# All page loads of the first stage issued by GpSimd's queue instead of half by GpSimd and half by SyncE

## The chip, the cores and the metric

The kernel runs on one core of one Trainium2 chip. The metric is the device time of one execution in microseconds (us). Engines are named as the profile names them: PE is TensorE's matmul, PEld its weight load, DVE is VectorE, ACT is ScalarE, POOL is GpSimd, SP is SyncE. SP does no arithmetic here: its program only waits on semaphores and issues DMAs. All DMAs, whoever issues them, are carried out by the core's 16 DMA engines; the profile calls SP's queue q1, POOL's queue q0 and ACT's queue q10.

## What is computed (the reference)

One inference step of two layers: a convolution mixer, then an attention layer over a paged cache. Only the past cache and the mixer's input product matter here; the reference, cut to that:

```python
def conv_mixer(x, state, w_in, ...):            # layer 0
    h = x @ w_in + b_in                         # 1024 -> 3 x 2048
    ...                                         # gate, 31 taps, layer norm, gate, product

def compress(kseq, pe, w1, b1, w2):             # layer 1, of keys and of values
    chunks = kseq.reshape(B, nchunk, 16, N_KV, HEAD_DIM)
    parts = einsum("bcsgd,jsdh->jbcgh", chunks, w1r)
    ...
    return einsum("bcgh,hd->bcgd", silu(h), w2)

past = cache_kv[page_table].reshape(8, 2048, 4, N_KV, HEAD_DIM)   # 8 sequences of 16 pages
kc = compress(past[:, :, 0], ...)
vc = compress(past[:, :, 1], ...)
cache_win_sample = concatenate([cache_win, new])[:, 8:]           # windows moved on by 8 rows
```

## The kernel before, in words

Each engine's program is written out by hand, with semaphores between them. The first stage runs 17 units, `u` from 0 to 16. In unit `u` PE multiplies channel tile `u` of the mixer (64 matmuls at L1385, weights `wi` of buffer `u % 2`), and beside it compresses "half sequence" `cu = u - 1`: the keys (even `cu`) or the values (odd `cu`) of one of the 8 sequences. A unit has 8 steps `q`. In each step ACT first gathers rows of the half sequence from the landing buffer `xc` (`regroup`, L791), PE transposes them (`turn_chunk`, L1428), ACT copies the result out of PSUM (`chunk_out`, L781), and PE multiplies it by the compressor's weights (L1456). ACT works two steps ahead: step 6 of unit `u` already gathers step 0 of the half sequence `cu = u`. That first gather waits for all 16 pages of the half sequence. Within a step PE's order is fixed: transposes, then the mixer's part, then the compressor's part, so PE stands still when ACT does.

A half sequence is 16 page loads of 128 KB, each to 8 partitions of `xc`, which has two buffers (`cu % 2`). A buffer is free once ACT has gathered the last step of `cu - 2` (`rg_ready`, 8 counts for a half sequence). Before the change two queues load it. POOL issues pages 8 to 15 as soon as the buffer is free (L700 to L708). SP issues pages 0 to 7 (`load_chunks`, L481), for `cu` 0 and 1 ahead of its loop, and then inside its loop over `u`. In the loop, L517 on, SP waits for the end of PE's unit `u` (`a_ps`), loads the weights and the state of unit `u + 2` (`load_mixer`, L471 and L473), stores the states of unit `u - 1` (L492, L493), waits for the buffer and issues its 8 pages of `cu = u + 1` (L485). In turn `u = 2` it issues two DRAM to DRAM copies after that: L531, 1408 KB of `state_conv`, and L533, 8064 KB of `cache_win`. What SP issues behind them runs in the same queue behind them.

At the very start ACT's queue loads the inputs, SP's queue loads the page table, `wi` of unit 0 and ten small tensors (L497 to L505, semaphore `s_small`), then the compressor's weights (L509), then pages 0 to 7 of `cu = 0`, `wi` of unit 1 and pages 0 to 7 of `cu = 1`. POOL's queue carries pages 8 to 15 of both from the start on. PE needs the ten small tensors before its first transposes of parameters (L1377), and these before unit 0.

Of the kernel before, what the change touches and what calls it, by code (L numbers as in the profile page):

```python
# [18 lines left out]
NB, TS = 8, 8  # L19
# [10 lines left out]
NPG = PAST // PAGE  # L30
STR = 16
# [18 lines left out]
STEPS = 8  # L50
# [45 lines left out]
def build_program(nc, x_prompt, x_sample, state_conv, cache_kv, cache_win, page_table,  # L96
# [4 lines left out]
    with ctx:  # L101
        def sem(name):
            return ctx.enter_context(nc.semaphore(name))

        arena = ctx.enter_context(nc.sbuf_tensor("arena", [P, ARENA], F32))
        pages = ctx.enter_context(nc.sbuf_tensor("pages", [1, NB * NPG], I32))
        bank = [ctx.enter_context(nc.psum_tensor(f"bank{i}", [P, 512], F32)) for i in range(8)]

        def at(kib, n):

            o = int(kib * 256)
            assert o + n <= ARENA
            return arena[:, o:o + n]
# [24 lines left out]
        xc = at(142, 2 * 4096).rearrange("p (c s f) -> p c s f", c=2, s=STR)  # L138
# [103 lines left out]
        s_cb = sem("s_cb")  # L242
        s_pg = sem("s_pg")
        xc_in = [sem(f"xc_in{c}") for c in range(2)]
        xq_in = [sem(f"xq_in{c}") for c in range(2)]
        rg_ready = sem("rg_ready")
        turn_ps = sem("turn_ps")
        turn_ev = sem("turn_ev")
# [215 lines left out]
        def _(sp):  # L464
            sp.dma_start(pages[:, :], page_table.rearrange("(o b) n -> o (b n)", o=1)).then_inc(s_pg, 16)

            def load_mixer(ct):
                c = ct % 2
                for a, part in ((0, 1), (1, 0)):
                    col = part * DIN + ct * P  # L470
                    sp.dma_start(wi[:, c, a], conv_w_in[0].rearrange("(k p) n -> p k n", p=P)[:, :, col:col + P]  # L471
                                 ).then_inc(wi_in[c], 16)
                sp.dma_start(st[0:120, c], state_conv[0].rearrange("(h b) t n -> (b t) h n", h=2)[:, :, ct * P:(ct + 1) * P]  # L473
                             ).then_inc(wi_in[c], 16)

            def load_gate(zi):
                col = 2 * DIN + zi * P
                sp.dma_start(wz[:, zi % ZS], conv_w_in[0].rearrange("(k p) n -> p k n", p=P)[:, :, col:col + P]
                             ).then_inc(wz_in[zi % ZS], 16)

            def load_chunks(cu):  # L481
                b, s = divmod(cu, 2)
                for n in range(NPG // 2):
                    pg = sp.value_load(pages[0:1, b * NPG + n:b * NPG + n + 1], min_val=0, max_val=cache_kv.shape[1] - 1)
                    sp.dma_start(xc[n * 8:n * 8 + 8, cu % 2],  # L485
                                 cache_kv[0, bass.ds(pg, 1)].rearrange("o (c s) k g d -> (o c) s (k g d)", s=STR)[:, :, s * 256:(s + 1) * 256]
                                 ).then_inc(xc_in[cu % 2], 16)

            def store_states(ct):
                c = ct % 2  # L490
                sp.wait_ge(turn_ev, TURN["tail", ct] + 1)
                sp.dma_start(state_p[0, 0, :, ct * P:(ct + 1) * P], uo[0:30, c, 0:P]).then_inc(state_out[c], 16)  # L492
                sp.dma_start(state_s[0, :, TAPS - 1 - TS:TAPS - 1, ct * P:(ct + 1) * P], uo[0:64, c, P:256]  # L493
                             ).then_inc(state_out[c], 16)
# [12 lines left out]
            def load_compressor():  # L507
                for s in range(2):
                    sp.dma_start(wc[:, s].rearrange("p j q h -> p (j q) h"),  # L509
                                 cmp_w1[0, s].rearrange("(q e) d h -> (e d) q h", e=2)).then_inc(s_wc, 16)  # L510

            load_compressor()
            sp.wait_ge(s_pg, 16)
            load_chunks(0)
            load_mixer(1)
            load_chunks(1)
            for u in range(CT):  # L517

                sp.wait_ge(a_ps, u + 1)
                if u + 2 < CT:  # L520
                    load_mixer(u + 2)
                else:
                    for zi in (2 * (u + 2 - CT), 2 * (u + 2 - CT) + 1):
                        load_gate(zi)
                if u:
                    store_states(u - 1)
                if 1 <= u < 2 * NB - 1:
                    sp.wait_ge(rg_ready, u * STEPS)
                    load_chunks(u + 1)
                if u == 2:  # L530
                    sp.dma_start(state_s[0, :, 0:TAPS - 1 - TS].rearrange("b t n -> b (t n)"),  # L531
                                 state_conv[0, :, TS:TAPS - 1].rearrange("b t n -> b (t n)")).then_inc(s_cpy, 16)
                    sp.dma_start(win_s[0, :, 0:WIN - TS].rearrange("b t k g d -> b (t k g d)"),  # L533
                                 cache_win[0, :, TS:WIN].rearrange("b t k g d -> b (t k g d)")).then_inc(s_cpy, 16)
# [41 lines left out]
            load_permuted(0, used + 24)  # L576
            load_compressor()

            sp.wait_ge(kv_out, 64)
            for st_ in range(2):  # L580
                for g in range(NKV):
# [36 lines left out]
            for n in range(NPG):  # L618
                pg = sp.value_load(pages[0:1, n:n + 1], min_val=0, max_val=cache_kv.shape[1] - 1)
# [48 lines left out]
        def _(pool):  # L668
# [30 lines left out]
            for cu in range(2 * NB):  # L699
                b, s = divmod(cu, 2)  # L700
                if cu >= 2:

                    pool.wait_ge(rg_ready, (cu - 1) * STEPS)
                for n in range(NPG // 2, NPG):
                    pg = pool.value_load(pages[0:1, b * NPG + n:b * NPG + n + 1], min_val=0, max_val=cache_kv.shape[1] - 1)
                    pool.dma_start(xc[n * 8:n * 8 + 8, cu % 2],  # L706
                                   cache_kv[0, bass.ds(pg, 1)].rearrange("o (c s) k g d -> (o c) s (k g d)", s=STR)[:, :, s * 256:(s + 1) * 256]
                                   ).then_inc(xq_in[cu % 2], 16)  # L708

            pool.wait_ge(hp_ev, 2)  # L710
            pool.memset(vbd, 0.0).then_inc(vbd_zero, 1)
# [54 lines left out]
        def _(act):  # L766
# [16 lines left out]
            def regroup(k):  # L783
                cu, q = divmod(k, STEPS)
                if q == 0:
                    act.wait_ge(xc_in[cu % 2], cu // 2 * 128 + 128)
                    act.wait_ge(xq_in[cu % 2], cu // 2 * 128 + 128)
                if k >= 2:

                    act.wait_ge(turn_ps, TURN["chunk", (k - 2) // STEPS, (k - 2) % STEPS] + 1)  # L790
                act.copy(rg[:, k % 2].rearrange("p g (e d) -> p g e d", e=2),  # L791
                         xc[:, cu % 2, 2 * q:2 * q + 2].rearrange("p e (g d) -> p g e d", g=NKV)).then_inc(rg_ready, 1)
# [117 lines left out]
            with act.Fori(0, 2) as it:  # L910
                for t in range(TT):
                    n = ROWS[t]
# [7 lines left out]
            for t in range(TT):  # L920
                n = ROWS[t]
# [28 lines left out]
            for gp in range(2):  # L950
                with act.Fori(0, 2) as it:
                    g0 = it * 32 + gp * 64
                    for u in range(33):
                        if u < 32:
                            n = (UNITS[u][1] + 1) * P
# [5 lines left out]
                        if u >= 1:  # L961
                            v = u - 1
                            n = (UNITS[v][1] + 1) * P
# [406 lines left out]
        def _(pe):  # L1370
# [328 lines left out]
            def step(b, c, scores=True, output=True):  # L1699
# [9 lines left out]
                def turn_weights(n):  # L1709

                    if n:
                        copied_out(n - 1)
                    pe.wait_ge(e_scl, b * 2 - (1 if n < 2 else 0))
                    for t, (col, rows, _) in enumerate(groups[n]):
                        last = pe.transpose(bank[7][0:rows, t * P:(t + 1) * P], p[:, col:col + rows], ident)
                    last.then_inc(e_pp, 1)

                def weigh(n):
                    copied_out(n)
                    if n == 0:  # L1720
                        pe.wait_ge(c_stage, b)
                        pe.wait_ge(v_in[s2], (b - 1 - s2) * 24 + 48)
                        pe.wait_ge(vp_in[s2], (b - 1 - s2) * 128 + 256)

                        pe.wait_ge(e_oz, b * 4 - 3)
                    for t, (_, rows, v) in enumerate(groups[n]):
                        for g in range(2):
                            rhs = pt[0:rows, n % 4, t * P:(t + 1) * P].rearrange("p (q g m) -> p g q m", q=TS, g=2)[:, g]
                            last = pe.matmul(bank[5 + g][:, 0:64].rearrange("p (q m) -> p q m", q=TS), v[:, g * P:(g + 1) * P], rhs,  # L1729
                                             start=n == 0 and t == 0, stop=n == 6)  # L1730
                    if n == 6:
                        last.then_inc(e_pv, 1)
# [98 lines left out]
```

## Time and profile before

| | us |
|---|---|
| median of 3 runs (1782.03 to 1786.17) | 1784.23 |
| the profiled execution, device time | 1785.66 |
| its span, from first to last instruction | 1784.1 |
| PE busy | 1642.5 (92%) |
| DVE busy | 875.2 (49%) |
| ACT busy | 498.4 (28%) |
| POOL busy | 179.9 (10%) |
| page loads of the first stage issued by POOL, and by SP | 128 each, of 128 KB |
| median from issue to landing, POOL's page loads (whole kernel) | 4.4 |
| median from issue to landing, SP's page loads (whole kernel) | 2.6 |

Times in the rows are from the start of the span. The busy share of an engine is an average over stages with different limits, so each stretch is read by itself. A landing is counted by the semaphore of a transfer, to which every DMA engine that took part adds; several loads in flight count on one semaphore, so a landing says when so many counts had come in, not which page it was.

### The profile page before, as it was taken

What the parts mean: (1) busy time and instruction counts of PE and PEld (TensorE: products, weight loads), DVE (VectorE), ACT (ScalarE), POOL (GpSimd) and SP (SyncE); (2) the same over time, 40 slices, a digit from 0 to 9 for tenths busy, and PEclk for the clock granted to TensorE, in tenths of its full rate; (3) what the DMA queues carried; (4) which work ended last, traced back from release to release, by engine and by line L of the source; (5) the groups of instructions that cost most, each with busy time, mean ns of one, the idle gap of its engine ahead of it and who ended that gap; (6) DMA issues with size and microseconds to landing.
All of it is one profiled execution on the core that took longest, in us unless ns stands there. A gap on an engine that the chain in (4) does not pass through costs nothing.

```text
span 1784.1 us, 24182 instructions
## 1 busy us (share of the span) xinstructions
PE 1642.5 (92%) x7065; PEld 1070.9 (60%) x7065; DVE 875.2 (49%) x1940; ACT 498.4 (28%) x1079; POOL 179.9 (10%) x336
## 2 busy tenths in 40 slices
PE   1999749999999999999989999997999979999897
PEld 1766536666666667743433366366778747777753
DVE  0467647888788754211320010016777763454334
ACT  0134223444444422210000000022666632333100
POOL 3012101111111000000000000002000024232100
PEclk6799969999999999999999999988999999999789
DMA  9557645766766526111002256103000045554501
GB/s 157 107 94 128 223 93 86 112 93 90 107 101 88 94 86 230 48 48 47 0 6 59 54 144 136 37 3 99 2 1 2 1 141 176 176 178 143 133 36 42
DMA packets 173096, 160.56 MB, mean 90 GB/s; under 512 B 55350, under 2 KB 150969, under 8 KB 172793
## 3 DMA queue, kind: packets, MB, share of 16 engines
q1 hardware_dynamic: 154742, 119.79, 29.9%
q0 software_dynamic: 16384, 33.64, 9.2%
q10 hardware_dynamic: 1864, 5.90, 0.9%
q8 instruction: 44, 0.72, 0.2%
q14 instruction: 62, 0.51, 0.1%
HBM read 152.41 MB, written 16.38 MB: 95 GB/s over the span
## 4 chain that ended last, share of the span: by engine, by line
PE 86%; SPq 4%; DMA 3%; DVE 2%; issue 2%; ACT 1%; POOLq 0%; POOL 0%; DVEq 0%; ACTq 0%
PE bank L1385 20%; PE bank L1456 11%; PE bank L395 11%; PE bank L1729 5%; PE bank L1664 4%; PE bank L1525 4%; PE bank L1801 4%; PE bank L1537 4%; PE bank L1688 4%; PE bank L1564 3%; PE bank L1428 3%; PE bank L1773 3%; PE bank L1678 2%; SPq L471 2%; DMA arena<-in_cmp_w_dram 2%
## 5 line engine op out<-in xcount | busy, mean ns | idle before, releaser
L1385 PE MATMUL bank<-arena 128*128 128x288 f32 x1536 | 401.1, 411 | 0.0
L1385 PEld LDWEIGHTS bank<-arena 128*128 128x128 f32 x1536 | 285.7, 193 | 69.1
L1065 DVE SCALAR_TENSOR_TENSOR arena<-arena 128x512 f32<-128x512 f32 x464 | 313.8, 743 | 0.0
L1456 PE MATMUL bank<-arena 128*128 128x508 f32 x512 | 238.8, 589 | 0.0
L395 PE MATMUL bank<-arena 128*128 128x512 f32 (+3 forms) x480 | 203.4, 571 | 2.7 <-DVE arena L1140 1.1
L781 ACT COPY arena<-bank 128x512 f32<-128x512 f32 x128 | 74.8, 585 | 297.0 <-PE bank L1428 297.0
L395 PEld LDWEIGHTS bank<-arena 128*128 128x128 f32 (+1 forms) x480 | 80.1, 194 | 125.6 <-issue 119.6
L1456 PEld LDWEIGHTS bank<-arena 128*128 128x128 f32 x512 | 97.3, 190 | 74.2 <-issue 60.8
L706 POOL DMA_DIRECT2D arena<-in_cache_kv_dram x128 | 76.6, 598 | 503.1 <-issue 502.9
L1428 PEld LDWEIGHTS bank<-arena 128*128 128x128 f32 x512 | 64.6, 143 | 91.6 <-issue 57.5
L1428 PE MATMUL bank<-arena 128*128 128x128 f32 x512 | 78.0, 275 | 32.4 <-ACT arena L808 32.4
L1729 PE MATMUL bank<-arena 128*128 128x64 f32 (+2 forms) x736 | 101.9, 295 | 5.6 <-DMA arena<-in_cache_kv_dram 5.6
L1729 PEld LDWEIGHTS bank<-arena 128*128 128x128 f32 (+2 forms) x736 | 98.0, 212 | 9.1 <-issue 7.7
L1664 PE MATMUL bank<-arena 128*128 128x128 f32 (+3 forms) x256 | 97.5, 468 | 1.6 <-DVE arena L1199 1.6
L791 ACT COPY arena<-arena 128x512 f32<-128x512 f32 x128 | 79.6, 623 | 45.0 <-DMA arena<-in_cache_kv_dram 45.0
L438 DVE SCALAR_TENSOR_TENSOR arena<-arena,bank 128x512 f32<-128x512 f32 (+1 forms) x20 | 13.6, 682 | 149.2 <-PE bank L1525 64.0
L1688 PE MATMUL bank<-arena 128*128 128x64 f32 x640 | 86.4, 267 | 0.0
L1688 PEld LDWEIGHTS bank<-arena 128*128 128x128 f32 x640 | 82.0, 193 | 2.1
L759 POOL DMA_DIRECT2D arena<-in_cache_kv_dram x128 | 70.9, 554 | 99.4 <-issue 99.2
L959 ACT ACTIVATE arena<-bank,arena 128x128 f32<-128x128 f32 (+3 forms) x128 | 67.7, 529 | 46.8 <-DVE arena L1237 45.6
L1773 PE MATMUL bank<-arena 128*128 128x512 f32 x160 | 76.7, 603 | 0.0
L1525 PE MATMUL bank<-arena 128*128 128x512 f32 (+1 forms) x160 | 74.2, 608 | 1.0 <-ACT arena L850 1.0
(213 smaller groups left out, 1819.1 us busy)
## 6 DMA issues: line engine op xcount, KB each, us to landing
arena<-in_cache_kv_dram POOLq DMA_DIRECT2D x256, 128.0 KB, 4.4
arena<-in_cache_kv_dram SPq DMA_DIRECT2D x256, 128.0 KB, 2.6
arena<-in_conv_w_in_dram SPq DMA_DIRECT2D x48, 512.0 KB, 7.1
arena<-in_nsa_w_in_dram SPq DMA_DIRECT2D x64, 128.0 KB, 2.3
arena<-in_cache_win_dram SPq DMA_DIRECT2D x16, 512.0 KB, 4.9
out_dram<-in_cache_win_dram SPq DMA_DIRECT2D x1, 8064.0 KB
arena<-in_nsa_w_in_dram SPq DMA_DIRECT2D x24, 256.0 KB, 2.6
arena<-in_conv_w_out_dram SPq DMA_DIRECT2D x2, 2048.0 KB, 8.1
```

The lines of the kernel that those rows point to most:

```text
L395: ins = pe.matmul(bank[t][0:r, 0:width], lhs(k, t), slot, start=first, stop=last_k)
L706: pool.dma_start(xc[n * 8:n * 8 + 8, cu % 2], cache_kv[0, bass.ds(pg, 1)].rearrange("o (c s) k g d -> (o c) s (k g d)", s=STR)[:, :, s * 2 ...
L791: act.copy(rg[:, k % 2].rearrange("p g (e d) -> p g e d", e=2), xc[:, cu % 2, 2 * q:2 * q + 2].rearrange("p e (g d) -> p g e d", g=NKV)).t ...
L1065: taps.append(ch.mark(dve.scalar_tensor_tensor(part, src, w, part, ALU.mult, ALU.add)))
L1385: last = pe.matmul(bank[pair + h][:, 0:HALF], weights[:, k], xT[:, k, h * HALF:(h + 1) * HALF], start=k == 0, stop=k == KT - 1)
L1428: last = pe.transpose(dst[:, g * P:(g + 1) * P], rg[:, k % 2, g], ident)
L1456: last = pe.matmul(h, wc[:, s, j, q], x4[:, :, j:j + NC], start=(q == 0 and j == 0), stop=(q == STEPS - 1 and j == 1))
L1525: last = pe.matmul(bank[t][0:r, :], y[:, c, t * P:t * P + r], wo[:, c], start=c == 0, stop=c == CT - 1)
L1664: pe.matmul(bank[u % 3][:, 0:n], qs[c][:, g2, i * P:(i + 1) * P], ktp[:, br, gp, 0:n], start=True, stop=True).then_inc(u_sc, 1)
L1688: last = pe.matmul(bank[5 + v % 3][:, 0:HD], probT[:, v % 2, k * P:(k + 1) * P], kvr[:, k, col:col + HD], start=k == 0, stop=k == i)
L1729: last = pe.matmul(bank[5 + g][:, 0:64].rearrange("p (q m) -> p q m", q=TS), v[:, g * P:(g + 1) * P], rhs, start=n == 0 and t == 0, stop=n ...
L1773: last = pe.matmul(s_bank[n][:, :], qb[:, c, g], ktb[n % 2][:, g], start=g == 0, stop=g == 1)
```

## The change

SP no longer issues page loads in the first stage: `load_chunks` and its three calls are gone, with the wait for `rg_ready` in SP's loop. POOL's loop issues all 16 pages of each half sequence, for the same `cu`, after the same wait as before. All 16 loads count on one semaphore, `xc_in`, and ACT waits for it alone. SP's wait for the page table moves to a later place, ahead of its first other use of pages.

```diff
-            def load_chunks(cu):
-                b, s = divmod(cu, 2)
-                for n in range(NPG // 2):
-                    pg = sp.value_load(pages[0:1, b * NPG + n:b * NPG + n + 1], min_val=0, max_val=cache_kv.shape[1] - 1)
-                    sp.dma_start(xc[n * 8:n * 8 + 8, cu % 2], ...).then_inc(xc_in[cu % 2], 16)
...
             load_compressor()
-            sp.wait_ge(s_pg, 16)
-            load_chunks(0)
             load_mixer(1)
-            load_chunks(1)
             for u in range(CT):
...
                 if u:
                     store_states(u - 1)
-                if 1 <= u < 2 * NB - 1:
-                    sp.wait_ge(rg_ready, u * STEPS)
-                    load_chunks(u + 1)
                 if u == 2:
...
                     pool.wait_ge(rg_ready, (cu - 1) * STEPS)
-                for n in range(NPG // 2, NPG):
+                for n in range(NPG):
                     pg = pool.value_load(...)
                     pool.dma_start(xc[n * 8:n * 8 + 8, cu % 2], ...
-                                   ).then_inc(xq_in[cu % 2], 16)
+                                   ).then_inc(xc_in[cu % 2], 16)
...
                 if q == 0:
-                    act.wait_ge(xc_in[cu % 2], cu // 2 * 128 + 128)
-                    act.wait_ge(xq_in[cu % 2], cu // 2 * 128 + 128)
+                    act.wait_ge(xc_in[cu % 2], cu // 2 * 256 + 256)
```

## Rows read from the trace of the kernel before

**Rows 1.** The page: PE's busy tenths in 40 slices of the span.

```profile
PE   1999749999999999999989999997999979999897
```

**Rows 2.** The chain that ended last, 170 to 252 us: start, length, what.

```profile
178.53 33.80 SPq L471
...
212.37 10.93 SPq L473
...
240.45 4.63 DMA arena<-in_cache_kv_dram
```

**Rows 3.** Timeline of PE, 205 to 252: start, length, instructions, idle before and releaser.

```profile
209.87 2.11 PE L1385 MATMUL bank<-arena 128*128 128x288 f32 x8
211.81 1.87 PE L1456 MATMUL bank<-arena 128*128 128x508 f32 x4
246.03 1.12 PE L1428 MATMUL bank<-arena 128*128 128x128 f32 x4 [32.35 <-ACT arena L808]
246.94 3.64 PE L1385 MATMUL bank<-arena 128*128 128x288 f32 x8
```

**Rows 4.** Timeline of ACT, around 172 and 245: gathers of the pages.

```profile
172.31 0.62 ACT L791 COPY arena<-arena 128x512 f32<-128x512 f32 x1
...
245.10 0.62 ACT L791 COPY arena<-arena 128x512 f32<-128x512 f32 x1 [38.74 <-DMA arena<-in_cache_kv_dram]
```

**Rows 5.** One unit's stretch: length, busy of each engine, granted clock, DMA share, GB/s.

```profile
306.00:340.00 34.00, 34.00 (x142) 22.70 (x141) 27.92 (x42) 14.28 (x26) 4.79 (x8) 1.00 0.71 97
```

**Rows 6.** Timeline of POOL: single page loads.

```profile
26.23 0.60 POOL L706 DMA_DIRECT2D arena<-in_cache_kv_dram  x1 [0.62 <-issue]
...
135.98 0.60 POOL L706 DMA_DIRECT2D arena<-in_cache_kv_dram  x1 [24.71 <-issue]
...
144.81 0.60 POOL L706 DMA_DIRECT2D arena<-in_cache_kv_dram  x1 [0.62 <-issue]
...
169.91 0.60 POOL L706 DMA_DIRECT2D arena<-in_cache_kv_dram  x1 [24.50 <-issue]
...
312.54 0.61 POOL L706 DMA_DIRECT2D arena<-in_cache_kv_dram  x1 [2.05 <-issue]
```

**Rows 7.** Line L706 alone: its 128 loads, from issue to landing.

```profile
DMA to landing us min/median/max: 4.2/5.4/44.2
```

**Rows 8.** Timeline of SP's queue, 140 to 180.

```profile
144.13 1.05 SPq L471 DMA_DIRECT2D arena<-in_conv_w_in_dram  x2
...
151.26 15.56 SPq L485 DMA_DIRECT2D arena<-in_cache_kv_dram  x8
166.87 0.73 SPq L531 DMA_DIRECT2D out_dram<-in_state_conv_dram  x1
...
178.06 34.27 SPq L471 DMA_DIRECT2D arena<-in_conv_w_in_dram  x2
```

**Rows 9.** DMA queues, 184 to 204: packets, MB, share of 16 engines.

```profile
q1 hardware_dynamic: 65, 4.19, 48.7%
q0 software_dynamic: 65, 0.13, 1.7%
```

**Rows 10.** DMA issues, 212 to 213: count, KB, us from issue to landing.

```profile
arena<-in_state_conv_dram SPq DMA_DIRECT2D x1, 120.0 KB, 18.8
```

**Rows 11.** Stretch 151 to 155, columns as in rows 5.

```profile
151.00:155.00 4.00, 4.00 (x18) 2.59 (x17) 4.00 (x5) 1.16 (x4) 0.00 (x0) 1.00 1.09 142
```

**Rows 12.** The chain, 0 to 82 us: the wait ahead of PE's first unit.

```profile
12.41 35.01 DMA arena<-in_cmp_w_dram
```

**Rows 13.** DMA queues in 36:41.8; then q1 in 41.8:44.8; in 44.8:47.6.

```profile
q0 software_dynamic: 256, 0.42, 62.8%
q1 hardware_dynamic: 7, 0.06, 5.0%
...
q1 hardware_dynamic: 19, 0.04, 3.8%
...
q1 hardware_dynamic: 32, 0.02, 2.7%
```

More of the change, by code:

```diff
@@ L244, in build_program @@
         xc_in = [sem(f"xc_in{c}") for c in range(2)]
-        xq_in = [sem(f"xq_in{c}") for c in range(2)]
         rg_ready = sem("rg_ready")
@@ L479, in load_gate @@
                              ).then_inc(wz_in[zi % ZS], 16)
-            def load_chunks(cu):
-                b, s = divmod(cu, 2)
-                for n in range(NPG // 2):
-                    pg = sp.value_load(pages[0:1, b * NPG + n:b * NPG + n + 1], min_val=0, max_val=cache_kv.shape[1] - 1)
-                    sp.dma_start(xc[n * 8:n * 8 + 8, cu % 2],
-                                 cache_kv[0, bass.ds(pg, 1)].rearrange("o (c s) k g d -> (o c) s (k g d)", s=STR)[:, :, s * 256:(s + 1) * 256]
-                                 ).then_inc(xc_in[cu % 2], 16)
             def store_states(ct):
@@ L577, in _ @@
             load_compressor()
+            sp.wait_ge(s_pg, 16)
             sp.wait_ge(kv_out, 64)
```

## The prediction

> **What bounds the kernel now.** I read PE's slices first [rows 1]: outside the stage changes PE is at 9 tenths or more nearly everywhere, so a change of page loads can move the time only where PE has a hole. In the first stage there are two, slice 0 and slices 4 and 5. Then the table of stretches, for a unit with no hole: PE is busy 34.00 of 34 us [rows 5], though both queues load pages there. Units like this (I looked at 306 to 340 and 578 to 612) can gain nothing.
>
> The hole in slices 4 and 5 is followed back in three views. PE ends a unit's compressor part at 211.81 + 1.87 = 213.7 and then idles 32.35 us behind ACT; its next eight mixer matmuls take 3.64 us where the same eight took 2.11, the clock having dropped in the idle time [rows 3]. I price the hole at 32.35 + 2 = 34.5 us. ACT itself waited 38.74 us for pages, to 245.10 [rows 4]. So a wait of ACT costs PE about 4 us less than its length. The chain names the cause [rows 2]: SP's queue stands 33.80 us in the second weight load of L471, 10.93 us in L473, and only then issues its pages, the last landing at 245.1. SP stood because, two DMAs earlier, it had issued the copies L531 at 166.87 and L533 [rows 8], and its queue has no room until they run dry. POOL's eight pages of that half sequence had been issued from 169.91 on [rows 6].
>
> The hole in slice 0 is one wait: PE's first parameter transposes wait for the last small load, issued 12.41, landed 35.01 us later, at 47.4 [rows 12].
>
> **The change, part by part.** *SP's 128 page loads go.* A batch occupies SP for 15.56 us [rows 8], but no engine waits on SP except where it is blocked: worth nothing in an ordinary unit, and if anything else were late on SP it would now come some 17 us sooner. The three waits that move or go cost nothing: ACT's two become one on the same event, the page table landed long before.
>
> *POOL issues 16 instead of 8.* The pace is (144.81 - 135.98) / 7 = 1.26 us a load, so 16 take 20.2, and 5.4 more to land [rows 6, 7]: 25.6 us. The window is one unit of 34 us plus the 4 us from the step that frees the buffer to the step that gathers, 38 in all [rows 4 to 6]: covered, by 12 us. If that cover were gone, each us over it would cost one us in 14 units. POOL has nothing else to do until after the stage, so nothing queues behind its waits.
>
> *The copies start sooner.* Without pages SP reaches L531 right after L493, at about 150 instead of 166.87. The transfers don't start 17 us sooner, though: the DMA engines are full to 155 with SP's weights and state of unit 4 (share 1.09 in 151 to 155 [rows 11]), and POOL's eight extra pages now fall into this stretch, 8 x 1.26 = 10 us more work. So they start between 17 and 0 us sooner than now; I take 8. How the copy behaves is shown by 184 to 204 [rows 9]: in 20 us SP's queue moved 65 packets of 4.19 MB / 65 = 64.5 KB at a DMA share of about a half, eight engines, so 20 x 8 / 65 = 2.46 us a packet; and POOL's queue moved 65 as well, one for one. The 8064 KB are 128 such packets, 16 for each of eight engines: 39 us, and 1408 KB at the same rate about 7 more. An estimate from rates: they end near 219 now (a start near 170 plus 46 and some), near 211 after.
>
> *What is late then.* Unit 5 needs the weights and state of L471 and L473, still behind the copies, and the pages of `cu = 4`, now all in POOL's queue. Now L473 is issued at 212.37 and lands 18.8 later, at 231.2, 12 after the copies' end [rows 2, 10]; the same offset gives 223. The pages, issued 169.91 to 190, are held by the copy on the eight engines and flushed after it, as now the last caught one landed 44.2 us after its issue [rows 7], and I put them at the same 223. PE stands from 213.7 to 223 and pays 2 us of low clock: 11.5 us for 34.5, a gain of 23. With copies 17 sooner the loss would be 2.5 and the gain 32; not sooner at all, 21 and 13.5.
>
> *The start.* Here the extra 2 MB of pages of `cu` 0 and 1 cost. The small loads run on few engines: in 36 to 41.8, with POOL's queue full everywhere (256 packets), SP's moved 7, 0.83 us each; once POOL's pages were through, the next 5.8 us moved 19 + 32 = 51 [rows 13]. POOL issued its 16th load at 26.23 [rows 6]; after the change 16 more follow at 1.26, to about 47, so its queue stays full past 47. If all 51 packets keep alternating with POOL's at the loaded pace (5.8 x 16 engines / 256 = 0.36 us a packet for 46 small ones, 0.83 for some 5 large): 16.6 + 4.1 = 20.7 instead of 5.8, +15. If the extra pages disturbed nothing, 0; a gain is excluded, since SP's queue up to the last small load is unchanged and only meets more traffic. Many of POOL's packets are nearly empty, and the last 32 of SP's took only 2.8 / 32 = 0.09 us a turn with POOL's still among them: at the mean of 0.09 and 0.36, 46 x 0.22 + 4.1 = 14.3, +8.5. I take +9. It moves PE's whole first unit and is hidden by nothing. The compressor's weights come later by the same amount and are needed later by the same amount.
>
> Sum: +9 - 23 = -14: 1785.66 - 14 = 1771.7 for the profiled execution. The median lies 1.4 lower: 1784.2 - 14 = **1770 us**. The bounds make 1784 - 32 = 1752 to 1784 - 13.5 + 15 = 1786.
>
> One rule speaks against POOL as issuer. In POOL's rows each load takes 0.60 us with gaps of 0.62, the longest gap shown 2.05 [rows 6], while DVE is busy 27.92 of 34 us [rows 5]. The Trainium skill ("SBUF — State Buffer", section "SBUF: two separate sides", the box on DVE blocking DMA) says that a DVE operation in a two-port mode keeps GpSimd from writing the descriptors of its DMAs, and gives about 3.1 us for one that takes 0.62 alone; by that, 16 loads would take some 50 us and overrun the window by 17 us or so. The trace disagrees so far.
>
> **The rivals.** *(a) The pages of `cu = 3` are caught: slower.* They are issued from 135.98 on, after the change to about 156, and gathered at 172.31 [rows 4, 6]. A caught page has some five packets in each of the eight engines' queues (an estimate: 128 KB in packets of 4 KB over 16 engines, and its counts), each waiting for one of 2.46 us: 12 us a page. One page still queued when the copies begin is covered, two or more are not; with four, the copies' 20 packets an engine are used up, and the pages land when the copies end. That needs copies at their earliest, the full 17 us, with POOL's pages held back by the weights. Then ACT waits from 172.3 to about 206, 33.5 us, PE 29.5; unit 5 is then covered. 34.5 - 29.5 - 9 = -4: 1788. For it: the second half of the pages meets the weight loads. Against: both queues take turns, so most pages should be through before SP's queue reaches the copies. *(b) The start is not held up*: the small loads are nearly through when POOL's extra pages come. -23: 1761. *(c) The change does not act*: the copies start no sooner and the start pays its full price, -13.5 + 15: 1786, no change that can be told. *(d) POOL's issues are starved by DVE.* If the gap of 2.05 were every gap, a load would take 2.66, 16 of them 42.6, and 48 with landing: 10 over the window in each of 14 units, 1924. Two gaps of the stage are that long.
>
> **How the numbers follow.** Forecast 0.55, almost all of it between 1758 and 1780; (a) 0.18; (b) 0.13; (c) 0.12; (d) 0.02. For the range I leave out (d) and the far ends of the others: 1756 to 1790. About 0.2%, 3.6 us, is what a measurement of this kernel can tell from no change. Faster: forecast and (b), 0.68. Same: (c), 0.12. Slower: (a) and (d), 0.20.
>
> **What would show it.** Right: PE's first transposes start near 56 instead of 47.5; L531 is issued some 17 us sooner relative to its unit; the hole ahead of unit 5 shrinks from 32 to about 10 us, ended by the weights and state or by POOL's pages at nearly the same time; units from 6 on stay at 34.0. Wrong: a new hole ahead of unit 4, behind a wait of ACT for pages near 180 (rival a); a first transpose still at 47.5 (b); batches of POOL longer than 38 us (d). The forecast fails most easily in where the copies start, since each us of it is a us of the hole ahead of unit 5, and copies that start too soon catch pages.

## The result, and the profile after

The change makes the kernel slower: 1796.26 us (median of 5 runs, 1794.34 to 1796.60) against 1786.17 for the kernel before beside it (1782.03 to 1790.39), a ratio of 1.0054 with a 95% interval of 1.0035 to 1.0074. Forecast were 1770 us, in a range of 1756 to 1790. The profiled execution's span went from 1784.1 to 1795.0 us. Line numbers below are those of the kernel shown: the kernel after has L692 for the page loads of POOL (L706 before), L470 and L472 for weights and state (L471, L473), L516 and L518 for the copies (L531, L533), L776 for the gather (L791), L1413 for PE's transposes (L1428), L1362 for the first parameter transposes (L1377) and L1370 for the mixer (L1385).

The page of after: PE's busy tenths in 40 slices. Beside [rows 1], slice 1 has fallen from 9 to 6, and slices 4 and 5, which were 7 and 4, are 3 and 9.

```profile
span 1795.0 us, 24182 instructions
PE   1699399999999999999989999997999979999898
```

The chain of after, from 0 to 95 us (to be read beside [rows 12]) and from 175 to 232 (beside [rows 2]): start, length, what.

```profile
10.99 49.41 DMA arena<-in_cmp_w_dram
60.45 1.92 PE bank L1362 x16
...
184.31 35.87 another core or an unknown queue
...
221.14 1.11 PE bank L1413 x4
```

The small load that ended at 47.4 us now ends at 60.4, and with it the start of PE's first unit comes 13.0 us later. The long piece at 184 is not named by the chain. The timeline of ACT around it, which answers to [rows 4], names it: start, length, instruction, idle before and releaser.

```profile
220.21 0.62 ACT L776 COPY arena<-arena 128x512 f32<-128x512 f32 x1 [35.33 <-DMA arena<-in_cache_kv_dram]
```

And the timeline of PE, which answers to [rows 3]:

```profile
221.14 1.11 PE L1413 MATMUL bank<-arena 128*128 128x128 f32 x4 [28.94 <-ACT arena L793]
```

This is not the hole of before grown shorter. It stands one unit earlier: ACT waits for the pages of `cu = 3`, ahead of unit 4, where the kernel before had them in time, and waits for nothing at `cu = 4`, where it used to stand 38.74 us [rows 4]. The step from one batch of POOL's loads to the next over the hole is 182.38 to 247.11 in the trace of after, 64.73 us; the same step of before, one unit on, is 203.86 to 272.33, 68.47; a unit without a hole makes 33.94. So the hole cost 34.5 us before and costs 30.8 now: a gain of 3.7 where 23 was forecast. Against it stand 13.0 at the start: 9.3 lost. At the end of the first stage the profiled execution is 8.7 us later than before. The span's difference is 10.9; the last 2 or so appear only in the last stage, after 1450 us, where nothing was changed, and can't be told from the spread of the runs.

Why the pages are late shows in the timeline of SP's queue, which answers to [rows 8]:

```profile
161.93 0.74 SPq L516 DMA_DIRECT2D out_dram<-in_state_conv_dram  x1
...
190.52 23.40 SPq L470 DMA_DIRECT2D arena<-in_conv_w_in_dram  x2
```

The line L692 alone, POOL's 256 loads from issue to landing, as in [rows 7]:

```profile
DMA to landing us min/median/max: 4.4/11.2/52.2
```

And the one load issued at 167.95, among the DMA issues: count, KB, us to landing.

```profile
arena<-in_cache_kv_dram POOLq DMA_DIRECT2D x1, 128.0 KB, 52.2
```

The unit before the copies begins 12.5 us later than before (POOL's batch at 148.45 instead of 135.98 [rows 6]), so the copies, which would stand at 179.3, are issued 17.4 us sooner within their unit. They fall into POOL's batch of `cu = 3`, 148.45 to 167.95, and its last load lands at 168.0 + 52.2 = 220.2, when ACT is released. Only the end of the batch is caught. The eight loads issued in 148 to 158, then the one issued in 165 to 166, as DMA issues of after:

```profile
arena<-in_cache_kv_dram POOLq DMA_DIRECT2D x8, 128.0 KB, 5.2
...
arena<-in_cache_kv_dram POOLq DMA_DIRECT2D x1, 128.0 KB, 14.0
```

Fourteen landings of the batch are in by 165.5 + 14.0 = 179.5. The load after them, issued at 166.74, takes 35.2 us, and the last 52.2. Units without a hole are what they were [rows 5]; the columns are the length, the busy time of PE, PEld, DVE, ACT and POOL with counts, the granted clock, the DMA share and GB/s.

```profile
320.00:354.00 34.00, 34.00 (x141) 22.68 (x140) 27.87 (x41) 14.28 (x26) 9.68 (x16) 1.00 0.82 98
```

### The profile page after: what moved, and what is told of

Same layout as the page of the kernel before. It is cut to its first block, busy times and chain, and to the rows that moved or that the text cites. A ratio compares the mean times of both kernels' runs of the same rounds, so it can differ in the third digit from the quotient of the medians.

```text
span 1795.0 us, 24182 instructions
## 1 busy us (share of the span) xinstructions
PE 1647.9 (92%) x7065; PEld 1074.5 (60%) x7065; DVE 875.6 (49%) x1940; ACT 498.1 (28%) x1079; POOL 259.8 (14%) x464
## 4 chain that ended last, share of the span: by engine, by line
PE 88%; DMA 3%; DVE 2%; another core or an unknown queue 2%; issue 2%; ACT 1%; SPq 1%; POOLq 0%; POOL 0%; DVEq 0%; ACTq 0%
PE bank L1370 21%; PE bank L1441 12%; PE bank L394 11%; PE bank L1714 5%; PE bank L1649 4%; PE bank L1510 4%; PE bank L1786 4%; PE bank L1522 4%; PE bank L1673 4%; PE bank L1549 3%; PE bank L1413 3%; PE bank L1758 3%; DMA arena<-in_cmp_w_dram 3%; PE bank L1663 2%
## 5 line engine op out<-in xcount | busy, mean ns | idle before, releaser
L1370 PE MATMUL bank<-arena 128*128 128x288 f32 x1536 | 399.9, 410 | 0.0
L1370 PEld LDWEIGHTS bank<-arena 128*128 128x128 f32 x1536 | 285.3, 193 | 68.7
L692 POOL DMA_DIRECT2D arena<-in_cache_kv_dram x256 | 154.6, 604 | 444.9 <-issue 444.8
L1413 PEld LDWEIGHTS bank<-arena 128*128 128x128 f32 x512 | 64.4, 143 | 88.0 <-issue 57.3
L1413 PE MATMUL bank<-arena 128*128 128x128 f32 x512 | 77.9, 275 | 28.9 <-ACT arena L793 28.9
L776 ACT COPY arena<-arena 128x512 f32<-128x512 f32 x128 | 79.6, 623 | 35.3 <-DMA arena<-in_cache_kv_dram 35.3
L745 POOL DMA_DIRECT2D arena<-in_cache_kv_dram x128 | 72.8, 569 | 97.4 <-issue 97.4
```

The lines of the kernel that those rows point to most:

```text
L692: pool.dma_start(xc[n * 8:n * 8 + 8, cu % 2], cache_kv[0, bass.ds(pg, 1)].rearrange("o (c s) k g d -> (o c) s (k g d)", s=STR)[:, :, s * 2 ...
L1370: last = pe.matmul(bank[pair + h][:, 0:HALF], weights[:, k], xT[:, k, h * HALF:(h + 1) * HALF], start=k == 0, stop=k == KT - 1)
L1413: last = pe.transpose(dst[:, g * P:(g + 1) * P], rg[:, k % 2, g], ident)
```

## The experiments

Two causes have to be held apart, the start and the copies, and for each the question is what would remove it. The working theory after the result: the start costs 13 us, because POOL's 16 extra pages share the DMA engines with the small tensors; the copies cost 31, because they catch the pages of `cu = 3`. The rival for each stands in the expectations.

**Without the copies.** Two runs leave the copies out, `e2` from the kernel after and `e3` from the kernel before. What is left of the difference is then the start.

```diff
-                if u == 2:
-                    sp.dma_start(state_s[0, :, 0:TAPS - 1 - TS]..., ...).then_inc(s_cpy, 16)
-                    sp.dma_start(win_s[0, :, 0:WIN - TS]..., ...).then_inc(s_cpy, 16)
...
-            sp.wait_ge(s_cpy, 112)
+            sp.wait_ge(s_cpy, 80)
```

> The changed kernel without the two DRAM to DRAM copies (they are left out, so the old rows of the two state outputs are missing). Theory (the hole ahead of unit 4 is pages of cu = 3 caught behind the copies' packets): no hole, ACT never waits for pages after unit 1, total 1796 - 31 = 1765 us. Rival (16 loads from one queue beside the weights are too slow for one unit, copies or not): a hole of 5 us or more stays and the total is 1770 to 1796 us.

> The kernel before without the two DRAM to DRAM copies (left out as in the run above). Theory: the hole ahead of unit 5 goes, total 1786 - 34 = 1752 us; the changed kernel without copies is then slower than this by the start alone, 12 to 13 us. Rival (POOL's 16 loads cost something in every unit): the difference between the two without copies is 16 us or more.

Measured: `e2` 1763.65 us (ratio to before 0.9869, 0.9853 to 0.9885), `e3` 1750.51 (0.9796, 0.9779 to 0.9812). Both came as expected. In neither has the first stage a hole, so 16 loads beside the weights are not too slow for one unit. PE's first transposes in `e2`, timeline of PE:

```profile
61.09 1.92 PE L1357 MATMUL bank<-arena 37*128 37x37 f32 x16 [46.80 <-DMA arena<-in_cmp_w_dram]
```

The unit in which after has its hole, as a stretch of `e2`:

```profile
190.00:224.00 34.00, 34.00 (x138) 22.58 (x137) 27.87 (x41) 14.34 (x27) 9.59 (x17) 1.00 0.76 99
```

`e2` less `e3` is 13.1 us, and the transposes start 13.2 apart (61.09 and 47.85): without the copies the change costs the shift of the start and nothing else. The copies cost the kernel before 1787.25 - 1750.51 = 36.7 us (1787.25 is the median of before beside these runs) and the kernel after 1796.26 - 1763.65 = 32.6. The change gains 4.1 there, beside the 3.7 read from the traces. The two terms of the prediction are the right two, with other sizes. That 13.1 - 4.1 comes near the 10.1 measured says nothing new: it is the difference of the same medians, but for 1787.25 in place of 1786.17. `e2` shows one more thing: with no copy in the way, POOL's loads still land late, in the landing line of its page loads.

```profile
DMA to landing us min/median/max: 4.3/11.1/34.9
```

**The start, taken back.** `e1` keeps the change and holds POOL's second batch until the small tensors are in. `e6` does it to the kernel before, for all of POOL's pages.

```diff
+                if cu == 1:
+                    pool.wait_ge(s_small, 160)
                 for n in range(NPG):                 # e1
...
             pool.wait_ge(s_pg, 16)
+            pool.wait_ge(s_small, 160)               # e6
             for cu in range(2 * NB):
```

> The changed kernel, except that POOL waits for the ten small tensors before it issues the 16 pages of cu = 1 (the pages of cu = 0 go out as before). Theory (POOL's extra pages hold up the small tensors at the start): PE's first parameter transposes are back from 60.5 to about 47.5 us, the hole ahead of unit 4 stays at some 29 us, total 1796 - 13 = 1783 us. Rival (the later start has another cause: SP's queue no longer interrupted by pages, or the compressor's weights): the transposes stay near 60 and the total at 1796 us.

> The kernel before, except that POOL waits for the ten small tensors before its first page load. Theory (turns with POOL's pages are what makes the small tensors late, in the kernel before too): PE's first parameter transposes at about 30 us instead of 47.5, some of it given back because the pages and the weights of unit 1 then come later, total 1787 - 16 = 1771 us. Rival (the small tensors are slow by themselves, behind inputs and weights): the transposes stay above 42 us and the total is 1785 us or more.

`e1`: 1788.86 us, ratio 0.9995 (0.9978 to 1.0012), 7.4 less than after. `e6`: 1779.40, ratio 0.9960 (0.9946 to 0.9974). The timeline of PE in `e1`:

```profile
48.78 1.92 PE L1364 MATMUL bank<-arena 37*128 37x37 f32 x16 [34.01 <-DMA arena<-in_cmp_w_dram]
...
212.00 1.11 PE L1415 MATMUL bank<-arena 128*128 128x128 f32 x4 [29.02 <-ACT arena L795]
```

The same in `e6`:

```profile
28.87 1.92 PE L1378 MATMUL bank<-arena 37*128 37x37 f32 x16 [13.19 <-DMA arena<-in_cmp_w_dram]
...
68.34 1.09 PE L1429 MATMUL bank<-arena 128*128 128x128 f32 x4 [9.09 <-ACT arena L792]
...
238.06 1.11 PE L1429 MATMUL bank<-arena 128*128 128x128 f32 x4 [32.00 <-ACT arena L809]
```

In `e1` the transposes are 11.7 us sooner than in after and the hole is untouched, 29.02. Some 2 us are given back at unit 1, where PE waits 1.04 for its state: POOL's batch of `cu = 2` comes at 105.30 instead of 114.49, 9.2 sooner. That POOL's pages make the small tensors late holds already of the kernel before: without any page of POOL's beside them the transposes start 18.6 us sooner in `e6`. But there the pages are then late, PE stands 9.09 and 1.98 us at unit 1, and 7.6 are left at `cu = 2` (94.42 instead of 102.03), about what the time shows. The expectations were 6 and 8 us too good; both left out what is late next.

**The hole, pages first.** `e4` lets SP wait, ahead of the copies, until the pages of `cu = 3` have landed. The forecast's own picture, pages through and a short hole ahead of unit 5, is then put to the test without the catch.

```diff
                 if u == 2:
+                    sp.wait_ge(xc_in[1], 512)
                     sp.dma_start(state_s[0, :, 0:TAPS - 1 - TS]..., ...).then_inc(s_cpy, 16)
```

> The changed kernel, except that SP waits until the pages of cu = 3 have landed before it issues the two copies. Theory (the pages of cu = 3 are caught only because the copies are issued while their last ones are still in POOL's queue): the hole ahead of unit 4 goes; a shorter one appears ahead of unit 5, where the pages of cu = 4 and the weights of unit 5 wait for the end of the copies, about 9 us; total 1796 - 31 + 9 = 1774 us. Rival (whenever the copies run, a batch of 16 pages behind them waits for their whole length): a hole of about 30 us ahead of unit 5 in place of that ahead of unit 4, total 1796 us.

Measured: 1804.76 us, ratio 1.0087 (1.0053 to 1.0121), slower than after by 8.5, with runs from 1798.01 to 1809.87. SP's queue in `e4`:

```profile
180.24 0.74 SPq L517 DMA_DIRECT2D out_dram<-in_state_conv_dram  x1
```

ACT's first gather of `cu = 3`, and the one that waits:

```profile
185.24 0.62 ACT L777 COPY arena<-arena 128x512 f32<-128x512 f32 x1
...
247.26 0.62 ACT L777 COPY arena<-arena 128x512 f32<-128x512 f32 x1 [27.97 <-DMA arena<-in_cache_kv_dram]
```

PE:

```profile
248.19 1.11 PE L1414 MATMUL bank<-arena 128*128 128x128 f32 x4 [21.58 <-ACT arena L794]
...
264.89 4.21 PE L1371 MATMUL bank<-arena 128*128 128x288 f32 x8 [15.59 <-DMA arena<-in_state_conv_dram]
```

Two readings. The pages of `cu = 3`, disturbed by no copy, are all in at 180.24, and the gather is due at 185.24: a cover of 5.0 us, where the prediction had 12. And with the hole ahead of unit 4 gone, the next half sequence is caught whole (ACT 27.97), and after it the weights and state behind the copies (15.59). PE stands 37.2 us in the two holes where after stands 28.94. The short hole of the forecast doesn't come about. The rival of the expectation, that the whole length moves on, came nearer, but with a hole of 21.58 us instead of 30 and a second one on top, so that its total of 1796 was missed too.

**The copies' packets.** If a caught page pays one packet of the copy per packet of its own, smaller packets must shorten the hole. `e5` describes the copies row by row without joining the axes; `e9` writes the window copy as two interleaved halves, whose runs are 8 KB.

```diff
-  win_s[0, :, 0:WIN - TS].rearrange("b t k g d -> b (t k g d)")        # after
+  win_s[0, :, 0:WIN - TS].rearrange("b t k g d -> b t (k g d)")        # e5
+  win_s[0, :, 0:WIN - TS].rearrange("b (m h t) k g d -> b m h (t k g d)", h=2, t=4)[:, :, h]   # e9, h = 0, 1
```

> The changed kernel with the two copies at the same place, but described row by row, so that the window's copy moves in packets of 2 KB instead of 64.5 KB. Theory (a caught page pays one copy packet of 2.46 us for each of its own, since the two queues take turns): with packets some thirty times smaller the pages of cu = 3 pass, the hole ahead of unit 4 goes, and only the weights of unit 5, in SP's queue behind the copies, are late by about 8 us: 1796 - 31 + 8 = 1773 us. Rival (it is the bytes of the copies that occupy the DMA engines, whatever their packets): a hole of some 30 us stays ahead of unit 4, total 1796 us.

> The changed kernel with the window's copy at the same place, but as two interleaved halves whose longest contiguous runs are 8 KB (blocks of four rows, every second block), so that its packets are 8 KB instead of 64.5 KB, on the same queue. Theory (a caught packet of POOL's waits for one packet of the copy): a packet then costs about an eighth of 2.46 us, the pages of cu = 3 land near 180 us, the hole ahead of unit 4 is under 5 us, the weights of unit 5 are still behind the copies and cost 5 to 10 us ahead of unit 5; total 1796 - 31 + 8 = 1773 us (more if packets of 8 KB make the copy itself longer). Rival (the bytes or the copies' hold on the engines matter, whatever the packets): hole of some 30 us ahead of unit 4, total 1796 us.

`e5`: 1797.60 us, ratio 1.0049 (1.0028 to 1.0070). It decides nothing, since the packets stayed as they were. DMA packets in 184 to 204, in after:

```profile
DMA packets 1235, 5.68 MB, mean 284 GB/s; under 512 B 390, under 2 KB 902, under 8 KB 1167
```

The same line of `e5`:

```profile
DMA packets 1223, 5.61 MB, mean 280 GB/s; under 512 B 396, under 2 KB 908, under 8 KB 1155
```

PE in `e5`:

```profile
219.41 1.12 PE L1412 MATMUL bank<-arena 128*128 128x128 f32 x4 [29.23 <-ACT arena L792]
```

1235 - 1167 = 68 packets of 8 KB or more in after, 1223 - 1155 = 68 in `e5`, and the same hole. `e9`: 1789.56 us, ratio 1.0016 (0.9998 to 1.0034), 6.7 less than after. ACT in `e9`:

```profile
186.19 0.62 ACT L778 COPY arena<-arena 128x512 f32<-128x512 f32 x1 [2.25 <-DMA arena<-in_cache_kv_dram]
```

PE in `e9`:

```profile
250.38 3.92 PE L1372 MATMUL bank<-arena 128*128 128x288 f32 x8 [24.73 <-DMA arena<-in_state_conv_dram]
```

SP's queue in `e9`:

```profile
189.59 36.36 SPq L470 DMA_DIRECT2D arena<-in_conv_w_in_dram  x2
```

With small packets the pages pass the copy nearly unhindered: ACT waits 2.25 us instead of 35.33, and PE not at all. That the packet is the price of a turn holds. But the 1773 expected was missed by 17: ahead of unit 5, where 5 to 10 us were expected, PE stands 24.73. In 184 to 204 SP's queue moves 3.33 MB, where in after it moves 4.58, and the weights behind the copies stand 36.36 us instead of 23.40. Whether the copies are slower because they now share with the pages, or because of the smaller packets themselves, these runs don't separate. The hole goes from the pages to the weights.

**The copies on another queue.** `e10` lets ACT issue them, at step 0 of unit 3, so that SP's weights are no longer behind them in one queue.

```diff
-                if u == 2:                      # SP's program: both copies go
...
+                    if u == 3 and q == 0:       # ACT's program: the same two copies
+                        act.dma_start(state_s..., ...).then_inc(s_cpy, 16)
+                        act.dma_start(win_s..., ...).then_inc(s_cpy, 16)
```

> The changed kernel with the two copies issued by ACT at the start of unit 3 instead of by SP at the end of its turn u = 2 (about the same time), in the same packets. Theory (turns are taken between queues on each DMA engine, so it doesn't matter which other queue holds the copies): the pages of cu = 3 are caught as before and the hole ahead of unit 4 stays at 25 to 32 us; total 1792 to 1800 us. Rival (POOL's pages are held up by SP's queue, its descriptors or its weight loads, and not by the copies' packets): the hole shrinks to under 10 us and the total to about 1773 us.

Measured: 1804.27 us, ratio 1.0088 (1.0059 to 1.0118). The queues in 184 to 204 (packets, MB, share of 16 engines):

```profile
q10 hardware_dynamic: 63, 4.06, 47.6%
q0 software_dynamic: 681, 1.10, 28.7%
q1 hardware_dynamic: 63, 0.03, 0.5%
```

PE in `e10`:

```profile
214.99 1.11 PE L1414 MATMUL bank<-arena 128*128 128x128 f32 x4 [21.99 <-ACT arena L789]
228.69 4.04 PE L1371 MATMUL bank<-arena 128*128 128x288 f32 x8 [12.59 <-DMA arena<-in_state_conv_dram]
```

SP's state load in `e10`:

```profile
159.02 51.08 SPq L472 DMA_DIRECT2D arena<-in_state_conv_dram  x1
```

ACT's queue moves 63 packets of 4.06 MB / 63 = 64.4 KB, and SP's exactly 63 beside it, of half a KB each. In [rows 9] the same had been seen between SP's and POOL's queue (65 and 65). So packets go one for one whichever of the queues holds the copy. POOL's 681 in this stretch can't be told apart by engine. The rival falls: ACT waits 28.38 us for POOL's pages though SP's queue holds no copy. But time and hole miss the expectation, 1804.27 above 1792 to 1800 and 21.99 below 25 to 32, because the edit did more than change the queue: ACT issues the copies at 155.46, ahead of SP's load of weights and state at 157.39, where SP in after issued them behind it, at 161.93. The state load now waits for the copies as well: two holes, 21.99 and 12.59, for one.

**Both causes out of the way.** `e7` is the kernel after with POOL held until the small tensors are in, and with the copies cut into one sequence for each turn from `u = 2` to 9. `e8` is the kernel before with the same two edits, so that the two differ by the change alone. The cut alters one thing more than the time of the copies: in 145 to 149 of `e7` SP's queue moves 1.23 MB, the 1184 KB of one sequence's copies and little else, at 86.5% of the 16 engines. The whole copy took 48.7% [rows 9]. So a copy of one sequence uses more than eight engines. Which of the two helps is not separated.

```diff
+            pool.wait_ge(s_small, 160)
...
-                if u == 2:
-                    sp.dma_start(...)          # state_conv, then cache_win, all 8 sequences
+                if 2 <= u < 2 + NB:
+                    sp.dma_start(state_s[0, u - 2, 0:TAPS - 1 - TS], state_conv[0, u - 2, TS:TAPS - 1]).then_inc(s_cpy, 16)
+                    sp.dma_start(win_s[0, u - 2, 0:WIN - TS]..., cache_win[0, u - 2, TS:WIN]...).then_inc(s_cpy, 16)
...
-            sp.wait_ge(s_cpy, 112)
+            sp.wait_ge(s_cpy, 336)
```

> The changed kernel, POOL held until the small tensors have landed, and the copies issued one sequence at a time in turns 2 to 9 of SP's loop, row by row. Theory: neither the start nor the copies cost PE anything beyond a start near 30 us; against the run without copies (1764 us) 30 us less at the start, some of it given back: 1740 us. Rival (copies of 1 MB a unit still hold up the pages of a batch of 16): holes of several us in each of units 3 to 10, total above 1760 us.

> The kernel before, POOL held and the copies spread as in the run above. Theory (with both collisions gone it doesn't matter who issues the pages): 1750 - 14 = 1737 us, within 6 us of the run above. Rival (SP's pages, 15.6 us of issue behind the weights, are now what is late): units longer than 34 us and 10 us or more above the run above; or the reverse, if POOL's 16 loads are what is late there.

`e7`: 1737.47 us, ratio 0.9725 (0.9689 to 0.9762), the fastest kernel of this study, 58.8 us below after and 49.5 below the median of before beside it (1786.95). `e8`: 1743.92, ratio 0.9762 (0.9736 to 0.9788). PE in `e7`:

```profile
28.02 1.92 PE L1362 MATMUL bank<-arena 37*128 37x37 f32 x16 [13.56 <-DMA arena<-in_cmp_w_dram]
...
63.87 1.09 PE L1413 MATMUL bank<-arena 128*128 128x128 f32 x4 [5.41 <-ACT arena L776]
```

A unit of `e7` with copies in it:

```profile
156.00:190.00 34.00, 34.00 (x137) 22.53 (x136) 27.94 (x42) 14.29 (x26) 9.62 (x17) 1.00 0.79 134
```

PE in `e8`:

```profile
67.69 1.09 PE L1428 MATMUL bank<-arena 128*128 128x128 f32 x4 [9.53 <-ACT arena L791]
...
376.55 0.66 PE L1428 MATMUL bank<-arena 128*128 128x128 f32 x4 [0.91 <-ACT arena L808]
```

`e7` adds up by its rows: the transposes 60.45 - 28.02 = 32.4 sooner, 5.4 of it given back at unit 1, and the hole of 30.8 gone: 57.8 for 58.8 measured. With both collisions gone the change itself, `e7` against `e8`, is a gain of 6.5 us by the medians, but the runs overlap (1733.20 to 1743.68, and 1742.64 to 1745.84), so its size is loosely known. The rows tell where it lies. `e8` stands 9.53 and 1.88 us at unit 1 where `e7` stands 5.41, and 0.91, 0.36 and 0.55 at three later units, where ACT waits some 7 us for pages: 7.8 us more in all, 6.0 of it at unit 1. The trace of `e8` puts all nine waits of ACT for pages, 56.8 us together, down to SP's loads and none to POOL's; why SP's are late, whether because it issues them last in each turn, is argued and not shown. The expectation of 1740 for `e7` was 2.5 us too high; that of 1737 for `e8`, within 6 us of `e7`, was just missed. So POOL as the only issuer is somewhat better when its pages wait for the start and the copies are spread, mostly by its first batch. Without the hold, `e2` and `e3` differ by the start alone. In the kernel as it stands any such gain is buried under the start and the hole.

## Why the prediction was wrong

**What bounds the kernel now** held. Both holes are where the time was decided; units without one stayed at 34.00 of 34; SP's loads going was worth nothing in an ordinary unit; and in `e7`, with the holes taken out, PE makes its units from 2 on without a wait.

**POOL issues 16 instead of 8: the issue right, the landing wrong.** The step that failed reads "20.2, and 5.4 more to land [rows 6, 7]: 25.6 us ... covered, by 12 us". Issuing takes what was said, (167.95 - 148.45) / 15 = 1.30 us a load. But in `e4`, where no copy disturbs it, the batch of `cu = 3` is issued from 148.92 to 168.39 and lands at 180.24, 12 us after its last load, in place of 5.4. The 5.4 is a median over loads most of which were through before SP's weights of the unit came (in before, POOL's eight ended at 144.81 [rows 6], SP's weights began at 144.13 [rows 8]). Half of the batch now runs beside the weights, which start at 156.59 in after: the eight issued in 148 to 158 land in 5.2 us by their median, one issued at 165.52 in 14.0. The median of all is 11.2, and 11.1 with no copy at all. The window was too long as well, by less: 185.24 - 148.92 = 36.3 us instead of 38, as [rows 4, 6] had it, 172.31 - 135.98. So 36.3 - 31.3 leaves a cover of 5.0 us. In ordinary units that is still enough; ahead of the copies it is not.

**The copies start sooner: about right.** Taken were 8 us, between 0 and 17. They are issued 17.4 sooner within the unit; SP's weight load behind them gets room at 190.52 + 23.40 = 213.9, against 212.3 + 12.5 = 224.8 by [rows 2], so they run some 11 us sooner.

**What is late then: the step that decided.** The text put the pages of `cu = 3` among the rivals with "most pages should be through before SP's queue reaches the copies", and priced a short hole of 11.5 us ahead of unit 5. Most were: fourteen landings of the 16 were in by 179.5, and two came at 201.9 and 220.2. Since a landing counts engines and not pages, two missing landings are 32 counts, on eight engines the parts of four pages (an estimate, if they are spread evenly). Most was not enough. Rival (a) had its point, "with four, the copies' 20 packets an engine are used up", its place and its size right: it gave ACT 33.5 and PE 29.5, measured were 35.33 and 28.94. (Its five packets a page on each engine are four by the page of before, 16384 packets of POOL's queue for 256 loads on 16 engines.) Its condition was taken to need the copies at their earliest; they ran some 11 us sooner, not 17, and with landing at 12 us that sufficed.

Nor would the forecast have come true with the pages through. In `e4` they are through, and the copies are issued 180.24 - 148.92 = 31.3 us after the batch's first load, where before had 166.87 - 135.98 = 30.9. That is the case which the prediction priced as "not sooner at all", with a loss of 21 us (its own terms make 231.2 - 213.7 + 2 = 19.5). PE lost 37.2. So "the same offset gives 223" and "I put them at the same 223" failed too: the state load issued at 225.73 comes 39 us later, at 264.9, against 18.8 in [rows 10], and the pages of `cu = 4` come at 247.3. That POOL's next two batches, issued from 182.84 and 216.79, stand in each other's and the state's way by then is argued and not tested. Some 46 us of copy on eight engines, worked out in the prediction, are longer than one unit of 34 us, and in `e4`, `e9` and `e10` whatever stood next to them, pages or weights, came late: PE lost 37, 25 and 35 us. The text asked when the copies end and not how long anything waits that needs those engines meanwhile.

**The start: the mechanism right, the size wrong.** Taken were +9 us, between 0 and +15; measured are 13.0. The price was taken as the mean of 0.09 and 0.36 us a packet. The queues after, in 41.8 to 59.2 in steps of 5.8 us (packets, MB, share), to be read beside [rows 13]:

```profile
q0 software_dynamic: 367, 0.60, 99.1%
q1 hardware_dynamic: 9, 0.05, 6.0%
...
q0 software_dynamic: 422, 0.68, 104.3%
q1 hardware_dynamic: 17, 0.01, 1.6%
...
q0 software_dynamic: 400, 0.69, 101.7%
q1 hardware_dynamic: 22, 0.01, 2.0%
```

48 packets in 17.4 us are 0.36 us each: the loaded price, which was to hand as the upper bound, holds until the end. The discount for POOL's nearly empty packets came from a stretch in which POOL's queue was running dry. It had moved 256 packets in the 5.8 us before [rows 13]; in 41.8 to 44.8 and 44.8 to 47.6 of before it moved these:

```profile
q0 software_dynamic: 20, 0.03, 3.0%
...
q0 software_dynamic: 26, 0.03, 3.9%
```

**POOL starved by DVE**, rival (d), did not show: POOL's load takes 0.60 us and never more than 0.86, the batch of 16 about 20, beside a DVE busy 8.31 of 10 us in this stretch of after, which lies within the batch:

```profile
155.00:165.00 10.00, 10.00 (x41) 6.63 (x40) 8.31 (x14) 4.82 (x8) 4.57 (x8) 1.00 1.08 129
```

The Trainium skill ("SBUF — State Buffer", section "SBUF: two separate sides") gives about 3.1 us for a load that a DVE operation in a two-port mode keeps waiting. The trace of after has no such load beside the DVE operations of this stage; whether they are of the kind that the page means, no run here shows.

**The sum.** By its own terms with the measured sizes: +13.0 for +9, and -3.7 for -23, is +9.3 for -14, beside 10.1 measured. Of the error of 24 us, 19 lie in the hole, 4 in the start. The chance of 0.18 for rival (a) was too low because the prediction took the landing from the old company of the loads.

## What to carry to other kernels

A landing time is a property of its company: when loads are moved onto one queue or later in a unit, take their landing from a stretch where the new neighbours run, not from the median of the old one. When a bulk transfer moves forward, ask which loads are in flight at its new place, and compare its whole length on the engines that it uses with the time between two deadlines; if it is longer, moving it only chooses what is late, as in the places tried here, and it is better cut up, as in `e7`. Small tensors on which the first work depends go through before bulk loads are let loose.

## What the runs showed of the hardware

The window's copy moves in packets of 64.5 KB, 2.46 us each on eight engines (both worked out from [rows 9]). A queue that meets them there gets about one packet for each, whether SP's or ACT's queue holds the copy: 65 and 65 between SP and POOL [rows 9], 63 and 63 between ACT and SP (`e10`). Writing the copy with more axes changes nothing as long as its data are contiguous (68 large packets in both); 8 KB runs do, and the pages' wait fell from 35.33 to 2.25 us (`e9`). Beside POOL's full queue SP's small loads took 0.36 us a packet. Holding the pages until these were through brought the first use 18.6 us forward in the kernel before (`e6`), and 32.4 in the kernel after (`e7`). Of POOL's pages in one batch, those issued ahead of SP's weight loads landed in 5.2 us, the last ones beside them in some 12 without a copy (`e4`).
